# Choosing the tokens of sixteen experts: low parts of the first weight chunks on another engine and at another place, indicator products on fp32r tiles

## What is computed

```python
cap = EC_CAPACITY_FACTOR * t_ // N_EXPERTS                  # 256
aff = jax.nn.softmax(jnp.einsum('btd,de->bte', h, w_router), axis=-1)
top_aff, top_idx = lax.top_k(jnp.swapaxes(aff, 1, 2), cap)
xe = h[bidx, top_idx]
hid = jax.nn.silu(jnp.einsum('becd,edf->becf', xe, w_gate)) * jnp.einsum('becd,edf->becf', xe, w_up)
ye = jnp.einsum('becf,efd->becd', hid, w_down) * top_aff[..., None]
return jnp.zeros_like(h).at[bidx, top_idx].add(ye)
```

## Time and profile before

| | |
|---|---|
| median of 3 runs | 3908.07 us (3908.01 to 3911.43) |
| span of the profiled execution, first to last instruction | 3905.5 us |
| TensorE busy | 3710.6 us (95%) |
| GpSimd busy | 866.0 us (22%) |
| end of the mixers, barrier | 2696 to 2699 us |
| softmax and search | 2699 to 2756 us |
| slots and lists of tokens | 2756 to 2777 us |
| barrier, `pick`, gather, transposes, low parts of the rows | 2777 to 2791 us |
| experts | 2791 us to the end |

### The profile page before, as it was taken

How to read it: one execution, slowest core, us unless ns; L and a number is a source line. 1 busy time by engine, 2 the same in 40 slices (tenths; PEclk the granted TensorE clock), 3 DMA queues, 4 the chain that set the end, 5 groups by cost and what they waited for, 6 DMA issues and landing times. The chain is left out here.

```text
span 3905.5 us, 55387 instructions
## 1 busy us (share of the span) xinstructions
PE 3710.6 (95%) x18304; PEld 2845.0 (73%) x18304; DVE 2266.5 (58%) x3464; ACT 1610.8 (41%) x2913; POOL 866.0 (22%) x809
## 2 busy tenths in 40 slices
PE   8999999999997999979999999896699999999998
PEld 2444446445775999968787878785588888888887
DVE  5655620255665999964535343444677767677774
ACT  5333321123664666643424242222244544444442
POOL 2889400002113666620000000002001000000100
PEclk9999999999998999999999999997799999999999
DMA  7444351103114433325434342344366666676663
GB/s 280 141 137 140 105 140 41 38 0 88 26 25 171 125 118 123 118 84 183 144 129 162 111 155 92 130 150 149 120 215 217 211 209 214 210 225 212 216 206 93
DMA packets 240182, 551.94 MB, mean 141 GB/s; under 512 B 38315, under 2 KB 99275, under 8 KB 237515
## 3 DMA queue, kind: packets, MB, share of 16 engines
q1 hardware_dynamic: 207964, 435.45, 34.3%
q0 software_dynamic: 32112, 115.11, 9.9%
HBM read 440.44 MB, written 99.68 MB: 138 GB/s over the span
## 5 line engine op out<-in xcount | busy, mean ns | idle before, releaser
L2930 DVE TENSOR_TENSOR sb_we_low<-sb_we,sb_we_high 128x1024 fp32r<-128x1024 f32 x377 | 458.3, 1223 | 121.5 <-ACT sb_we_high L2880 121.5
L2880 ACT ACTIVATE sb_we_high<-sb_we 128x1024 fp32r<-128x1024 f32 x377 | 392.2, 1048 | 142.3 <-PE ey L2844 142.3
L2284 DVE TENSOR_TENSOR sb_wm_low<-sb_wm,sb_wm_high 128x1024 fp32r<-128x1024 f32 x127 | 155.3, 1223 | 400.7 <-ACT sb_wm_high L2197 400.7
L329 PE MATMUL p_ps<-sb_hT,sb_ring 128*128 128x512 f32 (+1 forms) x960 | 373.4, 550 | 1.8 <-ACT sb_raw L462 1.8
L2829 PE MATMUL eg<-sb_xe_parts,sb_we_high 128*128 128x512 f32 x1024 | 373.3, 397 | 1.6 <-DVE sb_xe_parts L2925 1.6
L2829 PE MATMUL eu<-sb_xe_parts,sb_we_high 128*128 128x512 f32 x1024 | 371.9, 396 | 0.0
L329 PEld LDWEIGHTS p_ps<-sb_hT,sb_ring 128*128 128x128 f32 x960 | 181.8, 190 | 188.4 <-issue 180.8
L2139 PE MATMUL pg<-sb_hb_high,sb_wm_high 128*128 128x512 f32 x768 | 303.0, 394 | 9.4 <-DVEq L2256 5.4
L2141 PE MATMUL pg<-sb_hb_high,sb_wm_low 128*128 128x512 f32 x768 | 300.2, 391 | 0.0
L2140 PE MATMUL pg<-sb_hb_low,sb_wm_high 128*128 128x512 f32 x768 | 300.2, 391 | 0.0
L2828 PE MATMUL eg<-sb_xe_parts,sb_we_low 128*128 128x256 f32 x896 | 251.2, 280 | 0.0
(11 more groups left out here) (394 smaller groups left out, 8205.6 us busy)
## 6 DMA issues: line engine op xcount, KB each, us to landing
sb_we<-in_w_ex SPq DMA_DIRECT2D x384, 512.0 KB, 4.5
sb_wm<-in_w_gates SPq DMA_DIRECT2D x96, 512.0 KB, 3.6
sb_wrow<-in_w_mod_row POOLq DMA_DIRECT2D x64, 256.0 KB, 3.9
sb_wm<-in_w_br SPq DMA_DIRECT2D x32, 512.0 KB
sb_ring<-in_w_ch POOLq DMA_DIRECT2D x19, 512.0 KB, 4.8
sb_gr<-gc_d SPq DMA_DIRECT2D x36, 256.0 KB, 3.7
sb_lk<-k_d SPq DMA_DIRECT2D x36, 256.0 KB, 4.0
sb_lq<-q_d SPq DMA_DIRECT2D x36, 256.0 KB, 4.2
```

Source lines behind the costliest of these rows:

```text
L329: last = nc.tensor.matmul(ps[:, b % BANKS, 0:wd], w[:, kind, k], g.hT[:, k, t0:t0 + wd], start=(k == 0), stop=(k == KD - 1))
L2284: v.tensor_tensor(wl[n], w[n], wh[n], ALU.subtract).then_inc(s.wl, 1)
L2880: nc.scalar.activation(wh[:, n % CUT], w[:, n % RAW], ACT.Copy).then_inc(s.wh, 1)
L2930: v.tensor_tensor(wl[:, n % CUT], w[:, n % RAW], wh[:, n % CUT], ALU.subtract).then_inc(s.wl, 1)
```

## The change

GpSimd's list in `choose` is gone, and with it the semaphore `high` that released it. ScalarE's seven high parts stay where they are, without signals. In `experts`, VectorE's third semaphore addition is gone; in its place the seven subtractions stand in VectorE's list, as `low_chunk(0, n)`, behind the two `pick`s and ahead of `low_rows(0, 0)`. Their operands and type are those that GpSimd had. Apart from that, the tiles `c_at_hi` and `c_named` get the type fp32r, so both operands of the 32 products of line 2645 are fp32r. `c_at_lo` stays fp32.

```diff
-        at_hi, at_lo = (sbuf(nc, c, n, [P, 2, P, SUB]) for n in ("c_at_hi", "c_at_lo"))
-        named = sbuf(nc, c, "c_named", [P, 2, HT, 2, P])
+        at_lo = sbuf(nc, c, "c_at_lo", [P, 2, P, SUB])
+        at_hi = sbuf(nc, c, "c_at_hi", [P, 2, P, SUB], F32R)
+        named = sbuf(nc, c, "c_named", [P, 2, HT, 2, P], F32R)
...
-            @blk.gpsimd
-            def _(pool):
-                for n in range(LEAD):
-                    pool.wait_ge(s.high, n + 1)
-                    nc.gpsimd.tensor_tensor(g.wel[:, n], g.we[:, n], g.weh[:, n], ALU.subtract)
-
...
-                    nc.scalar.activation(g.weh[:, n], g.we[:, n], ACT.Copy).then_inc(s.high, 1)
+                    nc.scalar.activation(g.weh[:, n], g.we[:, n], ACT.Copy)
...
-                dve.sem_inc(s.wl, LEAD)
...
                 pick(0, 0, 0)
                 pick(1, 1, 0)
+                for n in range(LEAD):
+                    low_chunk(0, n)
                 low_rows(0, 0)
```

More of the change, by code:

```diff
@@ L2585, in choose @@
             tab[:, at:at + n] for at, n in ((K_SAME, P), (K_PRE, P), (K_BLK, P), (K_FOLD, HE), (K_SPR, SUB), (K_HI, SUB), (K_LO, SUB), (K_TOK, LT)))
-        s = sems(nc, c, "ch", "tab high own ex aff tr trc acc cnt cut tally lim sum off slot turned lohi hi lo st wt pick keep wide end mg")
+        s = sems(nc, c, "ch", "tab own ex aff tr trc acc cnt cut tally lim sum off slot turned lohi hi lo st wt pick keep wide end mg")
         with nc.Block() as blk:
```

## The result

The changed kernel takes **3924.79 us** (median of 5 runs, 3920.71 to 3934.04); the kernel before, run beside it, 3908.07 us (3906.91 to 3912.83). The ratio is 1.0039, 95% interval 1.0028 to 1.005: **slower by 0.4%**, some 15 us. I had forecast 3899.8 us, and 3897.8 to 3903.5 as the range. The profiled execution of the changed kernel has a span of 3919.2 us, against 3905.5 before; it is that of the fastest of the five executions (3920.71 us), so the traces explain 13.7 us of the loss.

A forecast was written before the change was run, and what follows sets the result against it. TensorE was taken to bound the experts, and a chain of short dependent steps the stretch ahead. Gains of 6.48 + 0.1 + 1.66 = 8.24 us took 3908.07 to 3899.8 us, range 3897.8 to 3903.5.

The forecast's parts named there:

- The expert stage keeps its length unless the change makes one of its inputs late: Expert stage: TensorE always busy, so time saved ahead of expert 0's first product passes one to one into the end.
- what would show it: Closing list of expected trace signs; its last: wrong altogether if the chain before 2791 us shrinks without the end following.
- The search: Eight search steps, slowed by GpSimd's subtractions, fall from 2.36 to 1.554 us each: gain 6.48 us.
- The fp32r products: Products of the token lists: only the last two remain behind ScalarE's last input, 0.72 us; gain 1.66 us.
- Rival 1: Token lists: fp32r gives nothing at 128 columns, leaving 6.58 us of gain, 3901.5 us; chance 0.33.
- what I had priced as a possibility: Line 2650's fp32 products: if TensorE's clock stayed at half, they would take 0.4 us more.
- The subtractions behind the copies: VectorE's seven subtractions take 8.06 us under cover of the gather and first transposes: cost 0.
- rival 2: Gather: VectorE and GpSimd block one another once each, subtractions end 2.0 us later, 3900.5 us; chance 0.08.
- Rival 3: Subtractions lock the gather out, everything behind 7.24 us late: 3908.7 us, or 3907.1 with fast products; chance 0.04.
- Rival 4: Expert 0: TensorE's clock rises some 3 us later than assumed, costing 1.5 us, 3901.3 us; chance 0.05.
- within 0.2%: Whole kernel: measured time differs from the kernel before by at most 0.2%, 7.8 us; chance 0.57.

The follow-up runs named there:

- e3: The changed kernel with 64 idle semaphore additions put into TensorE's list in the search steps: 3904.38 us, ratio 0.9985.
- e4: The kernel before with 192 idle semaphore additions in TensorE's list ahead of the expert loop: 3934.56 us, ratio 1.0061.
- e2: The kernel before with the fp32r tiles alone, the subtractions still on GpSimd in the search: 3936.40 us, ratio 1.0065.
- e5: The changed kernel with VectorE's subtractions moved into the search in 28 pieces, and 64 idle instructions on TensorE: 3906.94 us, ratio 0.9989.
- e10: The changed kernel with VectorE's subtractions moved into the search in 28 pieces, and 16 idle instructions on TensorE: 3905.41 us, ratio 0.9986.
- e9: The changed kernel with 16 idle semaphore increments on TensorE in the search: 3907.24 us, ratio 0.9988.
- e12: The changed kernel with 160 idle semaphore increments on TensorE in the search: 3908.88 us.
- e8: The changed kernel with 240 idle semaphore increments on TensorE in the search: 3908.59 us.
- e6: The changed kernel with 8 idle semaphore increments on TensorE in the search: 3934.48 us.

## Why the prediction was wrong

**"The expert stage keeps its length unless the change makes one of its inputs late": the step that failed.** No input was late. I had looked at what the stage waits for by semaphores and transfers, and at nothing by which an engine gets its own instructions. I did write that an fp32 product is two records and an fp32r product one, and used that for its duration only, not for the length of the program. The stage took 1130.5 us instead of 1114.0: 12.2 us of stalls, and the rest in products that run longer beside the stalls, 1.7 us of it by the lower clock behind the first one. e3 and e4 show the place of the loop as the cause. No rival of mine had it, and I gave slower by over 0.2% a chance of 0.02. The third had the right sign and the wrong mechanism: the gather wasn't locked out. The last sentence under what would show it, where the chain shrinks and the end does not follow, is what happened.

Ahead of the experts, term by term, from cuts that both traces have. The cuts are the first product of the lists (`pick_ps`), the first `c_kept` and the first gather instruction, then the transposes and the first expert product:

| stretch, us | before | after | gained | forecast |
|---|---|---|---|---|
| softmax to first `pick_ps` | 66.07 | 59.59 | 6.48 | 6.48 |
| to `c_kept` | 9.77 | 8.82 | 0.95 | 1.66 |
| to the gather | 5.04 | 5.33 | -0.29 | +0.1 |
| to the transposes | 6.37 | 7.45 | -1.08 | 0 |
| to the first expert product | 5.30 | 5.26 | 0.04 | 0 |
| sum | 92.55 | 86.45 | 6.10 | 8.24 |

**The search: right, and to the hundredth by luck.** The mechanism holds, but the hundredth is that of one execution: in e2 and e4, which have GpSimd's subtractions in the search as before, the same stretch takes 65.24 and 65.59 us and not 66.07, which would be gains of 5.65 and 6.00 us. One step of the changed kernel in the stretch where a step took 2.36 us before, and the start of the next:

```profile
2735.71 0.16 DVE L2673 TENSOR_SCALAR sb_c_drop<-cnt_ps 128x1 int32<-128x1 f32 x1 [0.68 <-PE cnt_ps L2625]
2735.90 0.16 DVE L2676 SCALAR_TENSOR_TENSOR sb_c_cand<-sb_c_cand,sb_c_drop 128x1 int32<-128x1 int32 x1
2736.10 0.48 DVE L2671 TENSOR_SCALAR_CACHE_REDUCE sb_c_more<-sb_aff,sb_c_cand 128x256 f32<-128x256 f32 x1
```

All steps are 1.55 us long, and the instruction that took up to 2.12 us takes 0.16. e5 adds that VectorE's own pieces in the same place cost nothing, so it was GpSimd's part and not the work.

**The fp32r products: mechanism right, size wrong.** Rival 1 is refuted: the fp32r form is faster at 128 columns. The last quarter of the changed kernel:

```profile
2767.41 1.22 DVE L2708 TENSOR_TENSOR sb_c_at_hi<-sb_c_hi,sb_ctab 128x1024 fp32r<-128x1024 int32 x1
2767.53 1.71 ACT L2613 ACTIVATE sb_c_named<-sb_c_at_lo,sb_ctab 128x256 fp32r<-128x256 f32 x4 [0.56 <-DVE sb_c_at_lo L2706]
2768.68 1.78 PEld L2640 LDWEIGHTS pick_ps<-sb_c_named,sb_c_at_hi 128*128 128x128 f32 x8 [0.49 <-DVE sb_c_at_hi L2708]
2768.68 1.97 PE L2640 MATMUL pick_ps<-sb_c_named,sb_c_at_hi 128*128 128x128 f32 x8 [0.30 <-DVE sb_c_at_hi L2708]
2770.69 0.49 DVE L2712 TENSOR_TENSOR sb_c_kept<-pick_ps,sb_ctab 128x128 f32<-128x128 f32 x2 [2.06 <-PE pick_ps L2640]
```

Eight products in 1.97 us: 0.24 us each at the lower clock, near my 0.22. The mis-sized term is what stands behind the last input. I let only the last two products follow ScalarE, 0.72 us. But none of a quarter's eight can start before its `c_at_hi` is there, at 2767.41 + 1.22 = 2768.63. VectorE then takes the result at 2770.69, 1.45 us after ScalarE's last `c_named` (2767.53 + 1.71 = 2769.24), twice my 0.72. That is the 0.7 us between 1.66 and 0.95.

**The clock stayed at half in the lists.** TensorE now pauses for 0.30 us between the quarters, and its products are at the lower level to the end. The products of line 2650 of before then took what I had priced as a possibility, and left out of the sum (first before, then after):

```profile
2776.39 0.62 PE L2650 MATMUL end_ps<-sb_ctab,sb_c_wide 128*128 128x16 f32 x4 [1.65 <-DVE sb_c_wide L2722]
2772.31 1.03 PE L2645 MATMUL end_ps<-sb_ctab,sb_c_wide 128*128 128x16 f32 x4 [1.65 <-DVE sb_c_wide L2717]
```

That is 0.4 us lost. The stretch from `c_kept` to the gather gained some 0.1 us elsewhere and lost 0.3 in sum.

**The subtractions behind the copies: hidden, but not free.** For VectorE all went as forecast: seven of 128x1024 in 8.03 us (8.06 forecast), ended ahead of everything that it had next, and not lengthened by the gather, so that rival 2 is refuted. What I had taken as a fixed cover was itself stretched. The changed kernel's timeline:

```profile
2775.07 8.03 DVE L2924 TENSOR_TENSOR sb_we_low<-sb_we,sb_we_high 128x1024 fp32r<-128x1024 f32 x7
2776.02 1.17 POOL L2774 DMA_INDIRECT sb_xe<-h_d,sb_ti  x1 [81.12 <-DVE sb_ti L2909]
2777.49 1.92 POOL L2774 DMA_INDIRECT sb_xe<-h_d,sb_ti  x1 [0.30 <-issue]
2783.44 1.78 SPq L2758 DMA_DIRECT2D sb_we<-in_w_ex  x4
2783.45 0.17 DVE L2914 COPY sb_ta<-sb_xe 128x2 f32<-128x2 f32 x1 [0.35 <-DMA sb_xe<-h_d,sb_ti]
```

GpSimd's two gather instructions take 1.17 and 1.92 us instead of 1.02 and 0.97, in all nine profiles with the subtractions there within 0.01 us, and in none of the five without. e5 and e10 show it from the other side. The rows that I had argued from the earlier trace rows are gathers beside single subtractions with pauses, not beside seven in a row. From the gather's start to the transposes it is 7.19 us in the mean of nine profiles (6.70 to 7.69) against 6.63 in the mean of five (6.37 to 7.00): 0.6 us as a mean, 1.08 in the pair of the table. Rival 3, locked out for 7 us, is refuted; about a tenth of it is real. The two instructions are 1.1 us longer together, and why only half of that shows in the mean is open.

**Rival 4, the clock of expert 0:** not in the changed kernel's profile, where the clock rose 1.2 us ahead of the first expert product (before: 1.1 us ahead). It is real all the same: e9 and e12 above.

Without the loop's displacement the kernel would have come to 3904.4 us (e3) or 3907.2 (e9): 0.12 to 0.15% faster than the kernel before beside them (3911.5 us), 4.4 to 7.1 us, where the traces' mean of 92.87 (before and e4) against 86.20 promises 6.7. That is the case "within 0.2%", to which I gave most of the chance, but for a kernel that I did not forecast.

## What to carry to other kernels

An edit can cost time in a loop that it doesn't touch, by moving it in the instruction memory: for this loop on TensorE of 1578 instructions the start decides whether it is fetched anew at every turn. So count what an edit adds or removes in instructions ahead of a hot loop, and count the loop in the trace from jump to jump, semaphore instructions too; look at the packets of the instruction queue and at the waits named issue behind the jump back; where they rose, a few idle instructions ahead of the loop put it right (16 were enough here).

A cover is work with a duration of its own, which may grow when something is put beside it: seven two-tensor instructions in a row on VectorE doubled a GpSimd instruction that single ones had left alone.

## What the runs showed of the hardware

- TensorE keeps a loop of 1578 instructions resident over its turns at four places within 256 (16, 64, 160 and 208 instructions more than in the changed kernel), where it touches seven blocks by the places worked out, and refetches it at three (0, 8 and 240), where it touches eight, in nine packets of 16 KB a turn. With 256 more it is as with 0.
- When it refetches, the first product that the second block holds starts 2.7 to 4.1 us after the turn's first (five kernels, 30 turns). Products ahead of the block's edge hide it: stalls of 12.2, 13.1 and 15.0 us in all with six products, 17.7 with two, 4.8 with fourteen.
- A stall of 2 to 3 us can cost as much again in clock: behind e2's first stall (2.7 us) the clock is at its lower level for 6.8 us, and the products fall back another 2.9 us. Of the six stalls of a kernel such a stretch follows none (e8), one (the changed kernel), three (e2), four (e4) or five (e6). In e6 TensorE is busy for 15 us more than before for the same products, and the stage's mean clock is 0.98:

```profile
2787.00:3932.00 1145.00, 1112.63 (x5872) 950.17 (x5872) 789.70 (x1042) 512.13 (x700) 79.64 (x62) 0.98 0.64 199
```

- Fp32r products of 128x128x128 follow one another every 0.24 us at the lower clock, one record each, where fp32 took two.
- An indirect gather's instruction on GpSimd takes 1.92 us instead of 0.97 beside VectorE's back-to-back subtractions, while VectorE's aren't lengthened at all.
